# Two orders of TensorE's work inside an attention slot: the next pair of heads' scores first or last

## The reference

```
A (8 heads): keys within 128 of the query, sink logit; softmax over 256 or 384 keys
B (4 heads): all 512 keys, plain softmax
C (4 heads): neighbourhood in a grid, learned bias; here as 512 keys with a masking bias
sc = q @ k.T * scale (+ mask/bias);  p = softmax(sc);  o = p @ v
```

## Time and profile before

| | before |
|---|---|
| median of 3 runs | 2949.22 us (2948.8 to 2956.56) |
| profiled execution: its time / its span | 2948.64 / 2947.1 us |
| mean granted TensorE clock | 0.923 |
| busy: PE, DVE, ACT, POOL | 88%, 44%, 28%, 9% |
| the four attention parts, about | 165 to 172 us each |

### The profile page before, as it was taken

How to read it: one execution, slowest core, us unless ns; L and a number is a source line. 1 busy time by engine, 2 the same in 40 slices (tenths; PEclk the granted TensorE clock), 3 DMA queues, 4 the chain that set the end, 5 groups by cost and what they waited for, 6 DMA issues and landing times.

```text
span 2947.1 us, 32119 instructions
## 1 busy us (share of the span) xinstructions
PE 2602.3 (88%) x10690; PEld 1643.1 (56%) x10690; DVE 1306.8 (44%) x2604; ACT 813.3 (28%) x1613; POOL 258.5 (9%) x242
## 2 busy tenths in 40 slices
PE   4898978899499999999979899698985999999994
PEld 1456755567445555555536577465772555555552
DVE  0445535465433444333425554346544344433344
ACT  0215423153122222222212343224321222222221
POOL 0011000120000000000000110002000000000001
PEclk8798988999699999999979898798976999999997
DMA  9502112300479999999990301203006899999994
GB/s 349 205 13 103 44 45 82 114 23 23 157 261 334 339 335 353 334 332 333 340 372 1 115 22 43 105 1 115 33 33 228 314 340 335 353 333 334 332 341 167
DMA packets 271598, 591.82 MB, mean 201 GB/s; under 512 B 6350, under 2 KB 6350, under 8 KB 270928
## 3 DMA queue, kind: packets, MB, share of 16 engines
q1 hardware_dynamic: 251328, 514.87, 47.9%
q0 software_dynamic: 15536, 58.59, 6.6%
q10 hardware_dynamic: 4608, 16.78, 1.6%
HBM read 552.46 MB, written 39.85 MB: 201 GB/s over the span
## 4 chain that ended last, share of the span: by engine, by line
PE 75%; DVE 8%; issue 7%; DMA 3%; ACT 3%; SPq 2%; POOL 1%; POOLq 0%; PEld 0%; ACTq 0%; DVEq 0%; PEldq 0%
PE bank L1250 30%; PE bank L1103 5%; PE bank L1154 5%; PE bank L1268 4%; PE bank L1267 4%; PE bank L1269 4%; PE bank L1133 4%; PE bank L1180 2%; PE bank L1142 2%; DMA ring<-in_w_ada 2%; PE bank L1182 2%; PE bank L1181 2%; PE bank L1200 2%; SPq L289 2%; PE bank L1099 1%
## 5 line engine op out<-in xcount | busy, mean ns | idle before, releaser
L1250 PE MATMUL bank<-ring,hT 128*128 128x512 f32 x2048 | 895.1, 595 | 6.5 <-DVE hT L924 6.5
L1250 PEld LDWEIGHTS bank<-ring,hT 128*128 128x128 f32 x2048 | 388.3, 191 | 472.7 <-issue 470.0
L953 DVE TENSOR_TENSOR ring_r<-ring,down_hi 128x1024 fp32r<-128x1024 f32 x256 | 293.3, 1218 | 0.0
L947 DVE TENSOR_TENSOR pbuf<-pbuf,bank 128x512 f32<-128x512 f32 x64 | 44.0, 688 | 558.0 <-PE bank L1250 558.0
L598 ACT ACTIVATE down_hi<-ring 128x1024 fp32r<-128x1024 f32 x256 | 248.9, 1046 | 97.4 <-DMA ring<-in_w_down 97.4
L1154 PE MATMUL bank<-V,pbuf 128*128 128x64 f32 x1664 | 232.1, 280 | 39.6 <-ACT pbuf L545 29.4
L1154 PEld LDWEIGHTS bank<-V,pbuf 128*128 128x128 f32 x1664 | 216.5, 200 | 58.2 <-ACT pbuf L545 43.2
L1103 PE MATMUL bank<-ring,hT 128*128 128x512 f32 x512 | 229.9, 604 | 0.0
L1267 PE MATMUL bank<-down_hi,hid_hi 128*128 128x512 f32 x512 | 206.7, 404 | 0.0
L1268 PE MATMUL bank<-ring_r,hid_hi 128*128 128x512 f32 x512 | 202.9, 396 | 0.0
L1269 PE MATMUL bank<-down_hi,hid_lo 128*128 128x512 f32 x512 | 201.2, 393 | 0.0
(11 more groups left out here) (171 smaller groups left out, 3277.5 us busy)
## 6 DMA issues: line engine op xcount, KB each, us to landing
ring<-in_w_gate SPq DMA_DIRECT2D x64, 2048.0 KB, 10.8
ring<-in_w_up SPq DMA_DIRECT2D x64, 2048.0 KB, 10.4
ring<-in_w_down SPq DMA_DIRECT2D x64, 2048.0 KB, 14.5
ring<-in_w_ada SPq DMA_DIRECT2D x24, 2048.0 KB, 16.5
ring<-in_w_in SPq DMA_DIRECT2D x16, 2048.0 KB, 19.6
ring<-in_w_out SPq DMA_DIRECT2D x8, 2048.0 KB, 10.1
X<-residual ACTq DMA_DIRECT2D x24, 512.0 KB, 3.3
residual<-X POOLq DMA_DIRECT2D x16, 512.0 KB, 2.9
```

Of the source, the lines that this page charges most:

```text
L953: dve.tensor_tensor(ring_r[4 + n // 4][:, kk:kk + 2, :], ring[4 + n // 4][:, kk:kk + 2, :], full(down_hi[n // 4][kk // 4][:, kk % 4:kk % 4 ...
L1250: ins = pe.matmul(bank[2 * (n % 2) + half][:, :], hT[j % 2][:, k, :], ring[n][:, k, :], start=(k == 0), stop=(k == KT - 1))
```

## The change

In each even slot the scores of units k and k+1 are issued after T(k-2) and PV(k-3), where they were issued ahead of them. Waits and operands stay as they were; the other engines' lists are the same. Side work still follows the slot.

```diff
                 for kind, i, k in schedule():
                     if kind == "slot":
-                        if k < UNITS and k % 2 == 0:
-
-                            if k >= 2:
-                                pe.wait_ge(probs_ready, k - 1)
-                            for v in (k, k + 1):
-                                grp, qp, g, kp, _, _, _ = unit(v % 16)
-                                lo, nb = keys(i, v % 16)
-                                rows = slice(HD * g, HD * g + HD)
-                                pe.matmul(bank[v % 3][:, 0:nb * P], qT[rows, qp, i * P:(i + 1) * P],
-                                          kT[rows, kp, lo * P:(lo + nb) * P], start=True, stop=True).then_inc(scored, 1)
                         m = k - T_LAG
                         if 0 <= m < UNITS:
...
                             ins.then_inc(pv_done, 1)
+                        if k < UNITS and k % 2 == 0:
+
+                            if k >= 2:
+                                pe.wait_ge(probs_ready, k - 1)
+                            for v in (k, k + 1):
+                                grp, qp, g, kp, _, _, _ = unit(v % 16)
+                                lo, nb = keys(i, v % 16)
+                                rows = slice(HD * g, HD * g + HD)
+                                pe.matmul(bank[v % 3][:, 0:nb * P], qT[rows, qp, i * P:(i + 1) * P],
+                                          kT[rows, kp, lo * P:(lo + nb) * P], start=True, stop=True).then_inc(scored, 1)
```

## The result

| | before | after |
|---|---|---|
| median | 2949.01 us (4 runs) | 3097.23 us (3086.77 to 3100.49, 4 runs) |
| ratio | 1 | 1.0493, 95% interval 1.0461 to 1.0525 |
| profiled execution: time / span | 2948.64 / 2947.1 us | 3086.77 / 3085.2 us |
| mean granted TensorE clock | 0.923 | 0.893 |

The kernel is slower by 148 us, 4.9%. The forecast was 3034 us with a range of 2980 to 3090: the direction was right, the 85 us forecast were a little over half of what came, and the range ended 7 us short of it.

A forecast was written before the change was run, and what follows sets the result against it. TensorE's list, work plus holes, was taken to bound the four attention parts. To 2948.64 us it added 65 for holes and 20 for the clock, giving a forecast of 3034 us, range 2980 to 3090.

The forecast's parts named there:

- The mechanism: Slots 10 and 11: ACT's copy stands behind exponentials, 3.21 us from scores to product; TensorE's hole becomes 1.65 us.
- The holes, 65 us: Four attention parts: TensorE's new holes after the scores add 16.2 us per part, 65 us in all.
- Bare pairs: Ten pairs, slots 2 to 20, almost without side work to fill the hole: 11.2 us more per attention part.
- pairs with a quarter: Nine pairs with a quarter of the output projection, which fills most of the hole: 3.5 us more per part.
- The pairs from slots 34 and 36: Among seven pairs with short side work, whose existing waits take up lateness: 0.15 us each, 1.0 us per part.
- from S(30) to S(34): End of a block: the new hole replaces DVE's old wait, 12.0 to about 12.2 us; 0.5 for two such places.
- The clock, 20 us: Attention parts: TensorE's clock falls in two more pairs per part, 5 us each part; bounds nothing and 100 us in all.
- My own sign of being wrong: Wrong if the parts' clock is below 0.85, waits shrink in number, or the copy starts under 2.6 us after the scores.
- The expected wait of 80 to 90 us: Idle time before the V product ending with ACT's copy, over the run: from 29.4 us to about 80 to 90.
- The faster one: ACT's copy is held by the transposes, so scores cover it and 29.4 us of waits vanish: 2920 us, chance 0.04.
- A loss that is swallowed by present waits: Existing waits and backlogs absorb all but the pairs of slots 2 to 16: loss 33, 2982 us, chance 0.26.
- The second one: The clock swings through all ten pairs of slots 2 to 20, 65 + 100 us: 3114 us, chance 0.12.

The follow-up runs named there:

- with both: Both orders, with ACT's copy ahead of the exponentials and DVE's copy ahead of the minimum: 2927.94 us in the old order, 2965.77 us in the new.
- the filler: Changed kernel plus an unread 128x512 matmul in 16 odd slots per attention part, ahead of the product waiting for ACT's copy: 3013.95 us, ratio 1.0211.
- ACT's swap: ACT's copy of unit k-2 put ahead of unit k's exponentials: changed kernel 2976.44 us; kernel before 2920.22 us.

## Why the prediction missed

*The bound.* Right: TensorE's list sets the length of an attention part, and the stretches outside moved by 1.6 us in all.

*The mechanism.* Right, to the hundredth for the pair it was drawn on: 3.21 us from scores to product, the hole larger, ahead of the same product. That the copy is late for its place behind the exponentials was shown twice by moving it: the changed kernel gains 121 us, the kernel before 28. It is not the whole cost of the order: 56 us of it stay with ACT's copy ahead, 38 with both.

*The holes, 65 us.* Near, and low if anything. With the clock held at its old level by the filler, the kernel stands 65 us above the one before (interval of the ratio 1.0186 to 1.0236, 55 to 70 us). That is a net figure, as the filler also costs something where it doesn't fit a hole and mends slots 4 and 5. The single pairs at the upper level are the finer reading. Bare pairs take 4.42, 5.52, 5.57, 5.56, 5.06 us (slots 8 to 16, with the filler in place) where my layout makes 4.5 for the first and 5.6 for the pair of slots 10 and 11, and the ten of them add some 11 us, as laid out (11.2); pairs with a quarter 6.41, 6.96, 7.00. Two terms were too small. The pairs from slots 34 and 36 take 6.13 and 5.55 us where they took 5.26 and 4.78, 0.8 more each, where I had put 0.15: in the first the late copy of ACT adds a hole of 0.91 us and doesn't hide in the router's wait, in the second a wait of 0.51 us for DVE's copy is new. And from S(30) to S(34) it is 12.3 us (315.22 to 327.53) where I had 12.2, but the 12.0 of the earlier trace rows that I set it against held a fall of the clock. In the other three parts before it was 11.5, as here in the second:

```profile
641.28 1.13 PE L1133 MATMUL bank<-kT,qT 64*128 64x512 f32 x4
...
652.74 0.92 PE L1133 MATMUL bank<-kT,qT 64*128 64x384 f32 x4
```

With the fastest pair of each slot in either order, over all parts and with the filler runs, the new order costs some 20 us a part, 80 in all, where I had 16.2 and 65. Of the 140 us that the four stretches grew in the profiled executions this leaves some 60 for the clock. Both are estimates.

*The clock, 20 us.* **This is the step that failed.** I had taken "5 us per part (two pairs more)", and the clock term measured 83 us by the filler, from 3014 to 3097, and some 60 by the single pairs: three to four times the 20. I had its ends, nothing and 100 us, the row with the fall in it, and a price per low pair of 2.5 us that was near (8.55 less 5.5 is 3.0). What I got wrong is how many pairs would be low. I reasoned from the mean clock that the parts had, that is from a kernel with one hole of 1.35 us and one of 1.11 in a part (slots 32 and 48), and counted the new falls as if each ended with its pair. After, a hole of 0.9 to 1.5 us stands in each of nine neighbouring pairs (slots 2 to 18), and a fall lasts: 14 us after 252 in the first part. The lower level took 51 us more of each part, not 10. My own sign of being wrong came in as well: three of the four parts have a clock below 0.85. The page on TensorE's clock gate that I weighed says of frequent short idling that throughput is "degraded by the re-throttle/re-warm cost paid between bursts" (the Trainium skill, "TensorE: Matmul & The Clock Gate", section "A second HAM failure mode: psum-queue depth-cycling"); the trace agrees, with 88 us at the lower level before and 293 after. I had written that by that rule the sum would lie nearer its upper bound of 100, and then gave that case 0.12. That case's 3114 us came nearest of all that I wrote down.

*The expected wait of 80 to 90 us* for ACT's copy came out at 59.7. Much of that is the same clock: at the lower level the scores and transposes take longer while ACT and DVE don't, so the hole shrinks from 1.49 to 1.07 us as the pair grows. A wait column that rises less than forecast while busy time rises at equal work is a sign of the clock.

*The rivals.* The faster one needed the copy to be held by the transposes; it was not, as the moved copy shows. A loss that is swallowed by present waits happened only at the ends of blocks. The second one was right that the clock goes lower through neighbouring pairs, but not through all the bare ones (the pair from slot 8 stayed up in three parts, those from 16 and 18 in two), and it also did outside them (the pairs from slots 34 and 36 of the second part took 8.60 and 8.52 us). Its sum, 3114, was near partly by luck, as the holes in it were too small and the clock in it too dear. And the upper end of my range, 3090, does not lie half way from 3034 to 3114, as I wrote; that would be 3074.

## What to carry to other kernels

- When two engines work in a ring, a move on one engine is priced by what stands ahead of the released instruction in the *other* engine's list. Here a copy whose input had long been ready stood behind work that waits for the instruction that was moved back; moving the copy up was worth 28 us in the old order, and it took the price of the new order from 148 to 56 us.
- Where TensorE is the bound, a hole costs its length and then perhaps as much again in clock, as here (65 and 83 us by the filler, some 80 and 60 by the pairs). Ten pairs with such holes in a row brought two thirds of the loss, so look for such rows of holes and not only for the sum of idle time, and if the removal is hard, try to fill them with unread matmuls: 64 of them saved 83 us here, and 4 per attention part, with the copy moved, made the best version (0.9824 of the time before).
- Read busy time at equal work beside the waits: it is where a clock loss shows.

## What the runs showed that I had not expected

- The clock fell with TensorE idle for no more than 1.5 us at a time, and then stayed at 1.2 GHz through some 14 us in most of which TensorE was busy (252 to 266 us).
- The effect of filling is graded over a run: no filler 3097, 128 columns 3057, 512 columns 3014 us.
- The same part of the same program can hold the lower level for different lengths: parts of 192.8 and 174.5 us in one execution of the kernel with the new order in bare pairs alone. The four runs of that kernel spread over 27 us, the 20 of the kernel before beside it over 19.
- Unread matmuls can be free: 64 of about 0.86 us each made the kernel before no slower (ratio 0.9981).
- A move that mends a changed kernel has to be tried on the unchanged one too: of the 121 us that ACT's swap won in the new order, 28 were to be had without it.
